# A first block of 352 tokens and later ones of 432, table stores from SyncE, first output chunks begun early: one layer of a hybrid encoder on one core

## The reference

```python
h = rmsnorm(x, norm_mix);  z = h @ w_in                     # 1536 columns: xl, gl, us
xc, new_conv = causal_conv(xl, conv_buf, conv_w, conv_b)    # 4 taps
r, ig = sigmoid(blockdiag(xc, wa) + ba), sigmoid(blockdiag(xc, wx) + bx)
a = exp(-8 * r * softplus(-lam));  b = sqrt(1 - a*a) * (ig * xc)
hl[t] = a[t] * hl[t-1] + b[t];  y_lru = hl * gelu(gl)       # RG-LRU
# S5: 32 groups of 16 inputs and 64 complex states, diagonal
s[t] = Lbar * s[t-1] + Bbar @ us[t];  ys[t] = Re(C @ s[t]) + d * us[t]
g = gelu(ys);  y_ssm = g * sigmoid(g @ w_glu + b_glu)
x = x + concat(rmsnorm(y_lru), rmsnorm(y_ssm)) @ w_out
h2 = rmsnorm(x, norm_ffn);  x = x + (silu(h2 @ w_gate) * (h2 @ w_up)) @ w_down   # d_ff 2816
y = rmsnorm(x, norm_final)                                   # also returned: conv, LRU and S5 states
```

## Time and profile before

| | us |
|---|---|
| median of three executions | 2335.99 |
| lowest, highest | 2334.59, 2338.13 |
| profiled execution, its own time | 2338.14 |
| span of its instructions | 2336.3 |
| TensorE, VectorE, ScalarE, GpSimd busy | 2218.3, 1538.7, 1091.2, 418.8 |

### The profile page before, as it was taken

The page is one execution under the profiler, slowest core; times in us unless marked ns, Lnnn a source line. Parts: engine busy times, 40 slices in busy tenths (PEclk is TensorE's granted clock), DMA queues, the critical chain, the costliest instruction groups (busy, mean ns, idle before and its releaser), DMA issues.

```text
span 2336.3 us, 30354 instructions
## 1 busy us (share of the span) xinstructions
PE 2218.3 (95%) x11650; PEld 2129.7 (91%) x11650; DVE 1538.7 (66%) x2581; ACT 1091.2 (47%) x1459; POOL 418.8 (18%) x483
## 2 busy tenths in 40 slices
PE   4886899999999999999999999999999999999996
PEld 2565799999999999999999999999999999999996
DVE  7576546587756656876666587756657875665544
ACT  3455334564634455654444654634455563432232
POOL 7622101024011101221020023111102321100001
PEclk9966899999999999999999999999999999999998
DMA  4852333545333545553353656334455653343331
GB/s 160 219 173 73 115 117 115 154 153 183 120 117 118 176 132 153 163 162 109 117 176 108 148 170 178 123 112 128 162 141 153 165 150 108 118 142 113 112 127 63
DMA packets 191120, 322.82 MB, mean 138 GB/s; under 512 B 82944, under 2 KB 121152, under 8 KB 190848
## 3 DMA queue, kind: packets, MB, share of 16 engines
q1 hardware_dynamic: 188608, 313.54, 44.3%
q0 software_dynamic: 2368, 7.34, 1.0%
HBM read 296.39 MB, written 26.53 MB: 138 GB/s over the span
## 4 chain that ended last, share of the span: by engine, by line
PE 86%; DVE 6%; POOL 3%; ACT 2%; issue 1%; DMA 1%; POOLq 0%; SPq 0%; DVEq 0%; ACTq 0%
PE acc L783 27%; PE acc L785 26%; PE acc L784 26%; PE acc L870 1%; PE acc L869 1%; PE acc L879 1%; PE acc L859 1%; POOL tmp L502 1%; DVE rstd L1049 1%; PE acc L841 1%; PE acc L848 1%; DVE w_hl L930 1%; DMA t_dram<-tq 0%; DVE bmt L930 0%; DVE act_hl L930 0%
## 5 line engine op out<-in xcount | busy, mean ns | idle before, releaser
L783 PE MATMUL acc<-act_hl,w_hl 128*128 128x416 f32 x2544 | 908.4, 357 | 15.9 <-DVE act_hl L930 15.6
L785 PE MATMUL acc<-act_hl,w_hl 128*128 128x416 f32 x2544 | 898.4, 353 | 0.0
L784 PE MATMUL acc<-act_hl,w_hl 128*128 128x416 f32 x2544 | 895.3, 352 | 0.0
L930 DVE TENSOR_TENSOR w_hl<-w_raw,w_hl 128x1024 fp32r<-128x1024 f32 x428 | 529.7, 1251 | 79.8 <-ACT w_hl L606 78.4
L783 PEld LDWEIGHTS acc<-act_hl,w_hl 128*128 128x128 f32 x2544 | 482.1, 190 | 28.2 <-DVE act_hl L930 12.8
L784 PEld LDWEIGHTS acc<-act_hl,w_hl 128*128 128x128 f32 x2544 | 482.3, 190 | 10.1 <-issue 5.2
L785 PEld LDWEIGHTS acc<-act_hl,w_hl 128*128 128x128 f32 x2544 | 481.8, 189 | 0.9
L606 ACT ACTIVATE w_hl<-w_raw 128x1024 fp32r<-128x1024 f32 x428 | 442.2, 1051 | 66.7 <-DMA w_raw<-in_w_ffn 37.8
L930 DVE TENSOR_TENSOR x_acc<-x_acc,acc 128x416 f32<-128x416 f32 x480 | 273.1, 586 | 213.4 <-PE acc L785 206.9
L502 POOL TENSOR_TENSOR tmp<-tmp 128x416 f32<-128x416 f32 x135 | 171.3, 1269 | 1118.5 <-ACT tmp L614 1110.0
L783 PE MATMUL acc<-ff_hl,w_hl 128*128 128x416 f32 x880 | 311.7, 354 | 14.0 <-DVE x_acc L930 12.0
(11 more groups left out here) (159 smaller groups left out, 1912.5 us busy)
## 6 DMA issues: line engine op xcount, KB each, us to landing
w_raw<-in_w_ffn SPq DMA_DIRECT2D x330, 512.0 KB, 3.7
w_raw<-in_w_in SPq DMA_DIRECT2D x60, 512.0 KB, 3.3
w_raw<-in_w_out SPq DMA_DIRECT2D x40, 512.0 KB, 3.3
s5y<-y_dram SPq DMA_DIRECT2D x80, 256.0 KB, 4.2
s5t<-t_dram SPq DMA_DIRECT2D x64, 162.0 KB, 3.8
s5v<-v_dram SPq DMA_DIRECT2D x80, 128.0 KB, 3.9
x_acc<-in_x SPq DMA_DIRECT2D x4, 1664.0 KB, 8.0
out_y<-x_acc SPq DMA_DIRECT2D x8, 832.0 KB, 6.5
```

The source lines that it names most:

```text
L783: pe.matmul(out, w(0), x(0), start=first, stop=False)
L784: pe.matmul(out, w(0), x(1), start=False, stop=False)
L785: return pe.matmul(out, w(1), x(0), start=False, stop=last)
L930: return v.tensor_tensor(out, x, y, op)
```

## The change

- Block 0 has T0 = 352 columns, blocks 1 to 4 have 432. The sum stays 2080, the number of blocks and of instructions per block too. Every access is cut to `width(b)`; S5 has 44 and 54 columns. Block 0 has its own views (`zs_first`, `u5_first`) and DRAM scratch.
- The stores of the S5 tables are new steps of SyncE: `cs` (of `c1`), `ks` (of `ck`), `vs` (of `bt`) and `tt` (of `tr`). GpSimd issues none of them any more. The buffers `tq` are doubled; the second set lies under `u5`, so `zl` of block 0 waits for all table stores before it loads `u5`.
- `wc`(0) to `wc`(5) convert the weights of `glu` and of `out` 0 to 3 of block 0 at places of their own, in the S5 phase; before, each came two or three units ahead of its use.
- `oa`(0) to `oa`(3): the first four chunks of block 0's `out` take their LRU rows (k 0 to 3) into banks 0 to 3 before the S5 rows are normed; `out` 0 to 3 then add k 4 to 7. The other chunks and blocks are as before.
- Norms: ScalarE reads the sum from the bank and takes the root of sum/n + epsilon at once; then VectorE takes the reciprocal. The pass of L1047 and one of the two handovers are gone.
- `FIRST` and `MIXER` have new orders, and `SECOND` is the order of block 1's mixer. The new `FIRST` begins x, pa, sq1 0 to 3, tb 0, n1, pq, ts 0, pb, h1 0, 1, tr 0, h1 2, 3, tb 1, us 0, pc, tt 0, ts 1, tr 1, tt 1, gl 0, c1 0, cs 0, c1 1, tb 2, us 1, ck 0, us 2, cs 1, gl 1, c1 2, cs 2, ks 0, us 3, ck 1, ts 2, ks 1, c1 3; further on stand bm 2, tb 3, vs 1, gl 3, kt, bm 3, and pl, tr 3, cv 0, tt 3, vs 3, zl, ga 0, xl 1, bx 0, cv 1, ga 1, s5 0.

```diff
-NB, T = 5, 416
+NB, T0, T = 5, 352, 432
 LAST = NB - 1
-TPL = SEQ - LAST * T
+TPL = SEQ - T0 - (LAST - 1) * T
...
+def width(b):
+    return T if b else T0
...
+NOWN, EARLY = 6, 4
+def early(kind, b, j):
+    return kind == "out" and b == 0 and j < EARLY
...
+                elif kind == "cs":
+                    sp.wait_ge(c1_done, j + 1)
+                    sp.dma_start(y_dram[:, j * GE:(j + 1) * GE, 0:P], c1t[j % 2][:, :, 1:9, :].rearrange("p g t h -> p g (t h)"))\
+                      .then_inc(c1_st[j % 2], 16)
+                elif kind == "ks":
+                    sp.wait_ge(kj_done, j + 1)
...
+                elif kind == "vs":
+                    sp.wait_ge(btT_done, 2 * (j + 1))
...
+                elif kind == "tt":
+                    for n, (done, src) in enumerate(((cos_done, 1), (sin_done, 2), (trho_done, 0))):
+                        sp.wait_ge(done, j + 1)
+                        sp.dma_start(t_dram[:, j * GE // 2:(j + 1) * GE // 2, n],
+                                     tq[j % 2][src][:].rearrange("p (t q) c -> p t q c", q=2)).then_inc(t_st[n][j % 2], 16)
...
+                    else:
+                        for n in range(3):
+                            sp.wait_ge(t_st[n][0], 32)
+                            sp.wait_ge(t_st[n][1], 32)
...
                     for n in range(3):
-                        if j:
-                            po.wait_ge(t_st[n], 16 * j)
+                        if j >= 2:
+                            po.wait_ge(t_st[n][j % 2], 16 * (j // 2))
...
-            def root(which, b):
-                act.wait_ge(rec_done, NORM_N[(which, b)] + 1)
-                act.activation(rstd[:], rstd[:], ACT.Sqrt).then_inc(rstd_done, 1)
+            def root(step):
+
+                bank, tk = wait_m(act, step), width(step[1])
+                act.activation(rstd[:, 0:tk], acc[:, bank, 0:tk], ACT.Sqrt, bias=sm(EPSC), scale=1.0 / (NCH[step[0]] * P))\
+                   .then_inc(m_freed(step), 1)
...
-                v.tensor_scalar(rstd[:], acc[:, bank, 0:T], 1.0 / (NCH[step[0]] * P), EPS, MUL, ADD).then_inc(m_freed(step), 1)
                 wait_evacuated(v, step)
-                v.reciprocal(rstd[:], rstd[:]).then_inc(rec_done, 1)
+                tk = width(step[1])
+                v.reciprocal(rstd[:, 0:tk], rstd[:, 0:tk]).then_inc(rstd_done, 1)
...
+                if step in PLACE and NRAW + NOWN <= PLACE[step] + LEAD_HI < NU:
                     weight_hi(PLACE[step] + LEAD_HI)
+                elif kind == "wc":
+                    weight_hi(NRAW + j)
...
+                elif kind == "oa":
+                    u = UNIT[("out", 0, j)]
+                    pe.wait_ge(w_lo, u - NRAW + 1)
+                    pe.wait_ge(kj_free, 2 * KL)
+                    pe.wait_ge(btT_done, 2 * KL)
+                    for k in range(KL):
+                        pe.wait_ge(nrm_lo, k + 1)
+                        three(acc[:, j, 0:tk], lambda s: w_hl[u % RING][:, s, k * P:(k + 1) * P],
+                              lambda s: act_hl[0][:, s, k, 0:tk], k == 0, False)
+                elif early(*step):
+                    u = UNIT[step]
+                    for k in range(KL, KD):
...
+                    ins.then_inc(early_full, 1)
```

More of the change, by code:

```diff
@@ L80, in steps @@
             if b + 1 < NB:
-                out += [(kind, b + 1, j) for at, (kind, j) in MIXER if at == place]
+                out += [(kind, b + 1, j) for at, (kind, j) in (MIXER if b else SECOND) if at == place]
     out += [("dn", NB * NPAIR - 1, h) for h in range(2)]
@@ L101 @@
 assert all(k in ("us", "xl", "gl") and not b for k, b, _ in SRC[:NRAW])
+NOWN, EARLY = 6, 4
+assert SRC[NRAW:NRAW + NOWN] == [("glu", 0, 0), ("glu", 0, 1)] + [("out", 0, j) for j in range(EARLY)]
+def early(kind, b, j):
+    return kind == "out" and b == 0 and j < EARLY
 PREP = {}
@@ L287, in wait_evacuated, with wait_row, zs, u5 @@
             eng.wait_ge(m_free[USE[key] % 3], USE[key] // 3 + 1)
+        def wait_row(eng, b, j):
+            if early("out", b, j):
+                eng.wait_ge(early_free, j + 1)
+            else:
+                wait_evacuated(eng, ("out", b, j))
+        def zs(b):
+            return zs_all if b else zs_first
+        def u5(b):
+            return u5_all if b else u5_first
+        def z_dram(b):
+            return z_all[b % 2] if b else z_first
+        def g_dram(b):
+            return g_all[b % 2] if b else g_first
         def chunk(b, i):
@@ L406, in _ @@
                         sp.wait_ge(kt_st, 16 * L)
-                        for n in range(3):
-                            sp.wait_ge(t_st[n], 64)
                         for gt in range(2):
@@ L837, in _ @@
                     if step == ("n1", 0, 0):
[L838 removed]
+                        pe.wait_ge(consts, 5)
                     pe.wait_ge(sum_done, SUM_AT[(kind, b)] + NCH[kind] - 1)
                     bank = m_bank(step)
[L841 removed]
+                    pe.matmul(acc[:, bank, 0:tk], ones[:], tmp[:, 2, 0:tk], start=True, stop=True).then_inc(m_full, 1)
                 elif kind in ("us", "xl", "gl"):
@@ L847, in _ @@
                                 pe.wait_ge(h_made, k + 1)
-                            ins = pe.matmul(acc[:, bank, 0:T], w_raw[UNIT[step] % RING][:, k * P:(k + 1) * P],
-                                            rows[:, k, :], start=k == 0, stop=k == KD - 1)
+                            ins = pe.matmul(acc[:, bank, 0:tk], w_raw[UNIT[step] % RING][:, k * P:(k + 1) * P],
+                                            rows[:, k, 0:tk], start=k == 0, stop=k == KD - 1)
                         ins.then_inc(m_full, 1)
@@ L1111, in _ @@
                 kind, b, j = step
-                if step in PLACE and PLACE[step] + LEAD_LO < NU:
+                tk = width(b // NPAIR if kind == "dn" else b)
+                if step in PLACE and NRAW + NOWN <= PLACE[step] + LEAD_LO < NU:
                     weight_lo(PLACE[step] + LEAD_LO)
+                elif kind == "wc":
+                    weight_lo(NRAW + j)
                 if kind in ("gate", "up", "dn"):
@@ L1152, in _ @@
                         for k in H_PARTS[j]:
-                            stt(rows[:, k, :], x_acc[0][:, k, :], v1(gain + k), rstd[:], MUL, MUL)\
+                            stt(rows[:, k, 0:tk], x_acc[0][:, k, 0:tk], v1(gain + k), rstd[:, 0:tk], MUL, MUL)\
                                 .then_inc(h_made, 1)
```

286 lines of the change are left out of this document (146 added, 140 removed).

## The result

The kernel before took 2337.06 us (median of four runs, 2334.59 to 2338.75), the changed one 2369.86 (four runs, 2365.55 to 2372.83): a ratio of 1.0139, 95% interval 1.0126 to 1.0151. The forecast was 2319 in a range of 2300 to 2339.

The account below looks back on a forecast made before the run. TensorE was taken as the bound from 284 us on, its matmul period set by columns. Terms of -38.1 us up to the FFN and +21 after it gave -17.1, from the median 2319 us, in a range of 2300 to 2339.

Parts of the forecast that it names:

- Step 8: Blocks 1 to 4 at 432 columns: 8448 matmuls at +0.0067 us each, +56.3 us (0 to +60.7).
- Step 7: Block 0 at 352 columns: glu and out -5.1 us, FFN -42.3, shrinking cover +5 (0 to 29).
- Step 10: Tail 0 us (-1 to +1); moves in later blocks' orders, under a TensorE that hardly waits, 0 (-4 to +6).
- steps 4 and 6: Norm waits between glu and out (-3.5 us) and from out to the FFN (-2.5); the root counted -1.05 in each.
- Step 1: Tables and start of S5: earlier stores bring the first state product to 112 us instead of 125.43, -13.5 us.
- Step 2: S5 phase, 125.4 to 193.8 us: shorter operations against four more weight conversions, -2 us (-7 to +5).
- Steps 3 to 7: To the end of out: wait before glu -1.5 us, glu-to-out wait -3.5, oa -10, glu and out width -5.1.
- Step 6: From out to the FFN, 267.72 to 284.01 us: shorter root and rows, -2.5 us (-1.5 to -3.5).
- A: Rival: matmul period fixed at 0.187 us at every width, so no width terms; 2305 us, chance 0.20.
- C: Rival: S5 doesn't start earlier, SyncE's one queue taking the place of GpSimd's; 2334 us, chance 0.18.
- B: Rival: VectorE with ScalarE can't follow in block 0's FFN, over 22 us new TensorE waits; 2343 us, chance 0.12.

Follow-up runs that it names:

- a432_32: Changed kernel (352 and 432 columns) with 32 bytes left free ahead of x_acc: 2348.05 us, ratio 1.0058 to the kernel before.
- b32: Kernel before with one line moved, buffer s5in laid ahead of u5, same instructions and order: 2347.22 us, ratio 1.0050.
- m3: Three-product matmuls alone in the act and ff patterns, packed rows moved by 0 to 800 bytes, wider strides too: act at 432 columns 195.2 to 197.7 ns.
- a416: Changed kernel with all widths back at 416 and 32 bytes left free ahead of x_acc: 2352.28 us, ratio 1.0072 to the kernel before.
- o416: As a416, with the blocks' orders also as in the kernel before, the prologue's new order kept: 2345.43 us, ratio 1.0044.
- p416: As o416, with s5in put back so that every buffer lies as in the kernel before: 2338.32 us, ratio 1.0008.
- q416: As p416, with the norms' roots as in the kernel before; new FIRST, SyncE's table stores, wc and oa remain: 2329.77 us, ratio 0.9981.
- qg416: As q416, with the 16 table stores of block 0 issued by GpSimd: 2332.19 us, ratio 0.9986 to the kernel before.
- qn416: As q416 without oa, all of block 0's out coming after the norm of the S5 rows: 2336.84 us, ratio 1.0004.
- z432: As q416, with widths 352 and 432 and 32 bytes left free ahead of x_acc: 2339.00 us, ratio 1.0017 to the kernel before.
- m1: Three-product matmuls alone at 13 widths, quiet, beside busy engines, beside loads, and with packed rows: 160.2 ns at 352 columns, 195.8 at 432.
- m2: Three-product matmuls alone at ten widths, packed rows moved by 0 to 96 bytes, then weights, then both: 159.1 to 163.2 ns at 352 columns.

## Why the prediction was wrong, step by step

The span grew by 27.4 us where the sum had -17.1. The difference of 44.5 lies in three places: 9.3 before the FFN, 9.5 in block 0's stage, 25.8 after.

- *Step 8, width of blocks 1 to 4, is the one that failed*: +56.3 forecast, 83 measured. It took (columns + 32) / 2.4 from one width and carried it to 432. The mechanism (columns set the pace) was right, the term was mis-sized by 3.1 ns a matmul: in the mean of a stream, 432 columns cost 194.9 to 197.9 ns by their place, and never 193.3. At the better place of `a432_32` the same 8448 matmuls cost 65 us more than before; so 9 of the missing 27 us are the width and 18 are the place. Its upper bound, proportion to 187, gave +60.7 and was too low as well. I had a second size in no trace of the kernel, and so no ground for bounds that narrow.
- *A term that was missing*: the place of the rows. The diff moves `s5in`, and I took that for bookkeeping. In the kernel before the move costs 11.5 us (`b32`). In the changed kernel it moves `act_hl` by 896 bytes and so leaves it at 32 modulo 128; what is bad there is the old place at the new width, and 32 bytes more take 19 us away (`a432_32`). What the move of `s5in` alone costs at 432 columns no run shows. From the places of `m3` with and without it (197.7 and 197.5 ns for `act`, 196.4 and 196.0 for `ff`) I estimate 2 us.
- *Step 7, block 0*: the FFN at 352 columns was right, 161.8 ns (`act_hl`) and 160.8 (`ff_hl`) where 160 was forecast, 1584 x -26.1 = -41.3. The cover did shrink: TensorE idles 11.8 us of that stage against 4.7, +7 where I had +5. The whole stage gained 24.3 of the 33.8 that steps 7 and 8 give for it. The spacing at 432 for block 1's input takes 1.6 of the difference, and the granted clock some 2: it stood at 1.2 GHz for 12.5 us of this stage, and for 7.8 before. Some 3 us are in no row that I can name.
- *Step 10, moves in later orders "0, -4 to +6"*: 6.5 to 7 us at 416 (`a416` to `o416`), just beyond its end.
- *The root* was counted as a saving of 1.05 us each in steps 4 and 6, and nothing after 284 us. In the blocks it costs 6 to 8.5 us (`p416` to `q416`): the pass that it saves VectorE had cost TensorE nothing (`q416` has it and no stall there), and ScalarE, with its order and its table loads, came into the chain.
- *Step 1*: first state product at 116.9, forecast 112, before 125.4. The wait before `c1`(2) went, and the next cover was the one named, `ck`(1):

```profile
69.45 1.36 DVE L1012 TENSOR_TENSOR c1t<-bb,pw 128x1152 f32<-128x1152 f32 x1 [6.74 <-PE acc L892]
...
79.43 3.27 DVE L1012 TENSOR_TENSOR rt<-bb,pw 128x1024 f32<-128x1024 f32 x1
...
111.70 0.17 DVE L1253 COPY xl<-conv_st 128x3 f32<-128x3 f32 x1 [5.17 <-ACT xl L770]
```

  The chain then ran through `bm` and xl 1. The four `bm` took 20.9 us where I had 15: most of their operations are slower than the 1.25 us that I counted, one takes 3.27, and GpSimd runs its last table round beside them, from 79.8 to 92.3. Behind them comes xl 1, whose copy VectorE awaited for 5.2 us: `ga`(1) at 114.4 is the branch that I had at 110 to 112. The loads of `u5` were issued at 105.9 to 109.9 and were not what was waited for. That the stores came early enough is due to the order more than to the engine (`qg416`: 1.6 us).
- *Step 2*: -2 forecast, +1.5 measured (69.9 us between first and last S5 product, 68.4 before).
- *Steps 3 to 7 up to the end of out*: last S5 product to the last of `out` took 53.4 us instead of 73.5, -20.1, and -1.5 - 3.5 - 10 - 5.1 is -20.1 too. That they agree to the tenth is luck: `oa` had 10 of it and is worth 7 (`qn416`), at the low end of its bounds, so the other parts gave more than forecast; which of them, no run shows.
- *Step 6*: -1.6 (8.2 us instead of 9.8 from `out` to the FFN), forecast -2.5. I dated the FFN's start by the row of 284.01, which is a later wait; its first product stood at 277.1, so 246 should have been 239. It came at 248.3. The stretch before it, with its wait:

```profile
240.19 0.32 PE L851 MATMUL acc<-act_hl,w_hl 128*128 128x352 f32 x1
242.65 0.86 PE L908 MATMUL acc<-tmp,ones 128*128 128x352 f32 x2 [2.15 <-POOL tmp L582]
248.34 0.63 PE L849 MATMUL acc<-act_hl,w_hl 128*128 128x352 f32 x1 [4.83 <-DVE act_hl L1012]
```

- *Rivals*: A (fixed period) is out. C is out: S5 started 8.5 us earlier. B named the right sign and the wrong mechanism: block 0 got 7 us of new waits, 12 in all, and B needed 22 new ones. No rival had the width's price or the place.

By ratios there are two ways from the kernel before (1) to the changed one (1.0139). The first goes over 416 columns: prologue, `oa` and stores -0.19%, roots +0.27, place of `ff_hl` +0.36, orders +0.28, place of `act_hl` net of `ff_hl` +0.25, widths +0.42. But its places are those of 416 columns, which the changed kernel doesn't have. The second keeps to the places at 432: prologue, `oa` and stores -0.19% (`q416`), widths at the better place +0.36 (`z432`), orders and roots together +0.41 (`a432_32` over `z432`), the bad place at 432 +0.81 (the changed kernel over `a432_32`). That is what the changed kernel pays.

What stays open: why the spacing rises above 400 columns and why the place matters. The steady patterns of the spacing, and the numbers that come back when rows and weights move together, look like two streams that meet, but no run here shows that.

## What to carry to other kernels

Price a new tile width by a short stream of the very matmuls that will run, at the very address and stride, before any order is planned on it: one width gives no slope, and 9 us a point told within 1 ns a matmul what 2300 us of kernel then did. A place that is good at one width can be the worst at the next, so the two are chosen together. When the pace of a bound engine differs at an unchanged shape, compare the buffer offsets; an allocation moved in a diff is a change of its own, and 32 bytes can be worth 19 us of 2370. An operation handed to another engine is priced by that engine's queue at that place (what stands ahead of it, table loads too), not by its own duration.

## What the runs showed of the hardware

- Three-product fp32r matmuls at 2.4 GHz: (columns + 32) / 2.4 ns up to 400 columns; 188.3, 193.1, 195.8, 200.0 ns at 416, 424, 432, 440 with rows 2048 bytes apart, 227 at 512 (`m1`). With packed rows the rise begins sooner: 182.1 to 182.9 ns at 400 (`m1`, `m2`), where the rule gives 180. No effect of a busy VectorE and ScalarE or of 393 GB/s of loads (`m1`).
- The spacing depends on the start of the moving rows modulo 128 or 256 bytes, and on that of the weights, by up to 4 ns of 187 (`m3`: ff at 416 columns has 186.7 to 191.0). The best place hangs on the width: rows at 32 modulo 128 in the `act` pattern are the best at 416 (187.9) and the worst at 432 (197.7, where 0 and 64 give 195.2).
- Plain float32 matmuls (two records of two passes) have in `m1` 295.8 ns a record at 352 columns, 349.2 at 416, 362.5 at 432 and 429.2 at 512, which is 2 x (columns + 3) / 2.4: no rise above 400, and a pass of 416 columns takes 174.6 ns where one of the fp32r form takes 186.7 at best.
